# Joint attention of a decoder step: eight identity products on TensorE ahead of each item's scores

## The chip, the cores and the metric

The kernel runs on one core of a Trainium2 chip. Times are microseconds (us) on the device for one execution, start to end. An execution under the profiler is a little longer than the others, so the trace's times are compared with its own total.

## The reference

One layer of a decoder, for a prompt of 1024 tokens and 8 sample tokens. What bears on the change is the dilated window attention: three head groups with (window, dilation) of (128, 1), (512, 4) and (2048, 16), four heads of 64 each, and their outputs combined by their softmax denominators.

```python
def masked_softmax_attend(s, valid, v, spec):
    s = jnp.where(valid, s, -jnp.inf)
    m = jnp.max(s, axis=-1, keepdims=True)
    e = jnp.exp(s - m)
    den = jnp.sum(e, axis=-1, keepdims=True)
    o = jnp.einsum(spec, e / den, v.astype(F32))
    return o, (m + jnp.log(den))[..., 0]
...
def combine_by_denominator(outs, lses):
    w = jax.nn.softmax(jnp.stack(lses), axis=0)
    return jnp.sum(w[..., None] * jnp.stack(outs), axis=0)
```

Ahead of it stands the input projection; behind it the stick-breaking attention, the gates and the output projection, and a mixture of 64 experts.

## The kernel before, in words

The phases run one after another, with all engines together at each border: the projection, `phase_windows` (the one that is changed), `phase_stick`, the gates, the output and routing, the experts. All is float32; large projections split operands into two fp32r parts, `phase_windows` multiplies float32 as it is.

`phase_windows` works on 24 items, one block of 128 queries of one head group each, for its four heads. Items 0 to 7 are of the group with dilation 16, 8 to 11 of the one with dilation 4, first half, 12 to 15 of the dense group, first half; 16 to 19 and 20 to 23 are the second halves. Items 0 to 12 have one block of keys (`nk` = 1, 128 columns), 13 to 23 two (256). Items of the dilated groups read their queries and keys from `turned` with a stride, the dense ones without.

Each engine has a program of its own, a loop over steps `i`, and semaphores order them. In step `i` TensorE writes the scores of item `i+1` (L1190), when DVE has taken those of item `i` out of the single buffer `pS` and masked them; then it transposes the weights of item `i-1` (L1200), when ScalarE has written the exponentials; then it multiplies those of item `i-2` with the values (L1211). In step `i` DVE masks item `i` (L1300), takes its maximum (L1305), which it may write only when the write of item `i-4` to DRAM has landed, since `packed` has four buffers (`PR`); then it negates it, copies the result of item `i-3` into `packed` (L1310), and does scores of the sample tokens in the first 17 steps (L1282, L1285). SyncE issues in step `i` the loads of item `i`'s values, the write of item `i-3`'s `packed` (L1153) and, in odd steps up to 13, four loads for a sample token.

When the last item that covers a tile of 128 tokens is through (item 12 for tile 0, `last_item[0]`), that tile's three parts are loaded (`comb`, L1379, GpSimd), weighed on DVE and ScalarE in step `last_item + 6` (L1361 on), shared out on DVE in step `last_item + 7` (L1352 to L1356), mixed on GpSimd (L1387 to L1394) and transposed on TensorE through `pM` in step `last_item + 9` (`TURN_M`, L1233). GpSimd loads tile t+2's parts after it has mixed tile t.

Of the kernel before, what the change touches and what calls it, by code (L numbers as in the profile page):

```python
# [13 lines left out]
P = 128  # L14
# [35 lines left out]
def rows_of(t):  # L50
    return P if t < NT - 1 else NS
# [19 lines left out]
def build(nc, a, o):  # L71
# [21 lines left out]
    with ExitStack() as ctx:  # L93
        sb = lambda name, shape, dt=F32: ctx.enter_context(nc.sbuf_tensor(name, shape, dt))
        held = []

        def semaphore(name):
            held.append(nc.alloc_semaphore(name=name))
            return held[-1]

        scratch["semaphore"] = semaphore
        ident = sb("ident", [P, P])
        expert_row = sb("expert_row", [1, NBLK + 1], I32)
        slot_info = sb("slot_info", [P, NBLK, 4], I32)
        with ExitStack() as attention:
            turned = attention.enter_context(nc.sbuf_tensor("turned", [P, 20, S], F32))
            phase_project(nc, a, o, scratch, ident, turned)
            branches = ctx.enter_context(ExitStack())
            odT = branches.enter_context(nc.sbuf_tensor("odT", [P, GW // P, T], F32))
            phase_windows(nc, a, o, scratch, ident, turned, odT)  # L110
            oT = branches.enter_context(nc.sbuf_tensor("oT", [P, SBH // 2, T], F32))
            phase_stick(nc, a, o, scratch, ident, turned, oT)

            nc.clear_and_free_semaphores(held)
            nc.all_engine_barrier()
            phase_gate(nc, a, o, scratch, turned, oT, odT)
            branches.close()
            phase_out_route(nc, a, o, scratch, ident, turned, expert_row, slot_info)
        phase_experts(nc, a, o, scratch, ident, expert_row, slot_info)
        phase_finish(nc, a, o, scratch)  # L120
# [869 lines left out]
def phase_windows(nc, a, o, sc, ident, turned, odT):  # L990
# [15 lines left out]
    last_item = [max(i for i, it in enumerate(items) if it["g"] == 0 and it["b"] == t) for t in range(NT - 1)] + [NI]  # L1006
# [8 lines left out]
    ZNEW, ZT, ZE, ZM, EM, SPV, VNEW, PACK, SPV2, PACK2 = 2, 18, 19, 20, 21, 22, 23, 23, 24, 25  # L1015
    WEIGH, MIX, TURN_M = 6, 7, 9
    STEPS = NI + TURN_M + 3

    def tokens(ap, it, first_block, blocks):

        v = ap.rearrange("p (l r) -> p r l", r=STEP[it["g"]])
        return v[:, it["r"], first_block * P:(first_block + blocks) * P]
# [6 lines left out]
    def tile_at(i, step):  # L1029
        return [t for t in range(NT) if last_item[t] + step == i]  # L1030

    with ExitStack() as ctx:
# [37 lines left out]
        pM = ctx.enter_context(nc.psum_tensor("pM_d", [P, 512], F32))  # L1070
# [47 lines left out]
        with nc.Block() as block:  # L1118
# [47 lines left out]
            @block.tensor  # L1166
            def _(pe):
                def sample_values(groups):
                    for g in groups:
                        for h in range(GH):  # L1170
                            for s in range(NS):

                                last = pe.matmul(pX[:NS, (g % 2) * GW + h * HD:(g % 2) * GW + (h + 1) * HD],
                                                 em[:, s, g * GH + h, :], vals[:, s, g, h * HD:(h + 1) * HD],
                                                 start=(s == 0), stop=(s == NS - 1))
                    last.then_inc(spv_done, 1)

                for i in range(-1, STEPS):
                    if i + 1 < NI:

                        it = items[i + 1]
                        g, nk = it["g"], it["nk"]
                        if i >= 0:
                            pe.wait_ge(s_masked, i + 1)
                        for h in range(GH):
                            b = 64 * (h % 2)
                            qt = tokens(turned[b:b + 64, 8 + 2 * g + h // 2, :], it, it["b"], 1)
                            kt = tokens(turned[b:b + 64, 14 + 2 * g + h // 2, :], it, it["b"] - nk + 1, nk)

                            last = pe.matmul(pS[:, h % 2, h // 2, :nk * P], qt, kt, start=True, stop=True)  # L1190
                        last.then_inc(s_ready, 1)
                    j = i - 1
                    if 0 <= j < NI:
                        nk = items[j]["nk"]
                        pe.wait_ge(e_ready, j + 1)
                        if j >= 1:
                            pe.wait_ge(eT_ready, j)
                        for h in range(GH):
                            for k in range(nk):
                                last = pe.transpose(pT[:, (h * nk + k) * P:(h * nk + k + 1) * P], e[:, j % ER, h, k * P:(k + 1) * P], ident[:, :])  # L1200
                        last.then_inc(eT_psum, 1)
                    j = i - 2
                    if 0 <= j < NI:
                        nk = items[j]["nk"]
                        pe.wait_ge(eT_ready, j + 1)
                        pe.wait_ge(v_in[j % 3], v_value[j])
                        if j >= 2:
                            pe.wait_ge(packed_ready, j - 1)
                        for h in range(GH):
                            for k in range(nk):  # L1210
                                last = pe.matmul(pO[:, j % 2, h * HD:(h + 1) * HD], eT[:, j % 2, (h * nk + k) * P:(h * nk + k + 1) * P],  # L1211
                                                 v[:, j % 3, k, h * HD:(h + 1) * HD], start=(k == 0), stop=(k == nk - 1))
                        last.then_inc(pv_done, 1)
                    if i == ZT - 1:
                        pe.wait_ge(z_ready, NU)
                        pe.transpose(pX[:NR, :P], z[:, :], ident[:, :]).then_inc(zt_psum, 1)
                    if i == ZM:
                        pe.wait_ge(se_ready, 1)
                        pe.transpose(pX[:, :NR], zt[:, :P], ident[:NR, :NR]).then_inc(e_psum, 1)
                    if i == SPV:  # L1220
                        pe.wait_ge(em_ready, 1)
                        pe.wait_ge(vals_in, 16 * NU)
                        sample_values((0, 1))
                    if i == SPV2:
                        pe.wait_ge(s_packed_part, 1)
                        sample_values((2,))
                    for t in tile_at(i, TURN_M):
                        m = rows_of(t)
                        pe.wait_ge(mixed_ready, t + 1)
                        if t:  # L1230
                            pe.wait_ge(odT_ready, t)
                        for c in range(2):
                            last = pe.transpose(pM[:, c * P:c * P + m], mixed[:m, t % 2, c * P:(c + 1) * P], ident[:m, :m])  # L1233
                        last.then_inc(mixed_psum, 1)

            @block.scalar
            def _(act):
                for i in range(STEPS):
                    if i < NI:
# [29 lines left out]
            def _(dve):  # L1269
# [17 lines left out]
                dve.wait_ge(consts_in, 32)  # L1287
                for i in range(STEPS):
                    if i < NI:
# [1309 lines left out]
```

## Time and profile before

| | us |
|---|---|
| median of 3 runs | 2373.95 |
| lowest, highest | 2372.28, 2374.68 |
| profiled execution, whole | 2383.18 |
| its span in the trace | 2381.4 |
| `phase_windows`, TensorE's first matmul to the next phase's first | 477.5 to 640.9 |

The span is what the trace covers, 1.8 us less than the whole. The change is in a stage of some 163 us, so it is read by windows and by the engines' timelines there, and not by the page's sums, to which the experts' stage gives most.

### The profile page before, as it was taken

The numbers are of one execution on the slowest core, as the hardware profiler recorded it, in microseconds if no ns is written. First come the engines' busy times: TensorE is split into PE (matmuls) and PEld (weight loads), VectorE is DVE, ScalarE is ACT, GpSimd is POOL, SyncE is SP. The second block draws the span as 40 slices with busy tenths as digits, with TensorE's granted clock in tenths as the row PEclk, the third lists the DMA queues.
The fourth block names the chain that finished last, engine by engine and source line by source line (L and its number), as shares of the span: only waits on it lengthen the run. The fifth ranks groups of instructions, "written<-read, shape, count | busy, mean of one in ns | idle before, by whom it ended". The sixth has DMA issues, their size and how long they took to land. (4 is left out here: it accounts for less than half of the span.)

```text
span 2381.4 us, 38212 instructions
## 1 busy us (share of the span) xinstructions
PE 2162.2 (91%) x13126; PEld 1578.2 (66%) x13126; DVE 1410.3 (59%) x2121; ACT 1037.4 (44%) x1563; POOL 1041.3 (44%) x824
## 2 busy tenths in 40 slices
PE   7999799879499988999899888999999999999994
PEld 6777677667344437888777545677667767767763
DVE  4487678767377753111357526666766766766772
ACT  6221122245266652111234105666666666666662
POOL 2111222122466650011006602677777776777762
PEclk9999899958699999999999898999999999999997
DMA  6577611064345528893352049999999999999995
GB/s 219 177 256 243 223 36 36 30 196 127 133 138 161 165 71 296 274 300 115 109 188 90 20 145 327 323 326 324 323 325 327 322 322 330 320 321 327 324 317 139
DMA packets 180334, 520.57 MB, mean 219 GB/s; under 512 B 22907, under 2 KB 78866, under 8 KB 153790
## 3 DMA queue, kind: packets, MB, share of 16 engines
q1 hardware_dynamic: 133654, 366.37, 44.7%
q0 software_dynamic: 36208, 93.16, 15.5%
q10 hardware_dynamic: 10368, 59.73, 7.5%
q8 instruction: 57, 0.93, 0.2%
q14 instruction: 47, 0.39, 0.1%
HBM read 442.31 MB, written 125.08 MB: 238 GB/s over the span
## 5 line engine op out<-in xcount | busy, mean ns | idle before, releaser
L2465 DVE TENSOR_TENSOR w_gu_lo<-w_e,w_gu_hi 128x2048 fp32r<-128x2048 f32 x132 | 301.9, 2287 | 37.5 <-ACT w_gu_hi L2391 32.7
L2391 ACT ACTIVATE w_gu_hi<-w_e 128x2048 fp32r<-128x2048 f32 x132 | 253.5, 1921 | 43.6 <-DMA w_e<-in_w_e_gate 41.5
L565 PE MATMUL pP<-wring,hT_hi 128*128 128x512 f32 (+2 forms) x576 | 229.4, 398 | 22.7 <-DVE wring L500 13.6
L2327 PE MATMUL pG_e<-w_gu_hi,xT_hi 128*128 128x512 f32 x528 | 232.7, 441 | 1.0 <-issue 1.0
L566 PE MATMUL pP<-wring,hT_hi 128*128 128x512 f32 (+2 forms) x576 | 224.2, 389 | 0.0
L567 PE MATMUL pP<-wring,hT_lo 128*128 128x512 f32 (+2 forms) x576 | 223.5, 388 | 0.0
L2327 PE MATMUL pG_e<-w_gu_hi,xT_lo 128*128 128x512 f32 x528 | 208.8, 396 | 0.0
L2327 PE MATMUL pG_e<-w_gu_lo,xT_hi 128*128 128x512 f32 x528 | 208.2, 394 | 0.0
L2260 POOL DMA_INDIRECT x_scratch<-y_e,target x66 | 107.6, 1630 | 190.4 <-ACT y_tail L2429 190.4
L2246 POOL DMA_INDIRECT rows_tail<-h_scratch,index x66 | 178.2, 2700 | 20.8 <-issue 20.8
L429 ACT ACTIVATE stage<-pP 128x512 f32<-128x512 f32 (+3 forms) x72 | 41.1, 571 | 312.2 <-PE pP L567 303.3
L341 POOL TENSOR_TENSOR wring<-turned,wring 128x512 fp32r<-128x512 f32 (+1 forms) x43 | 71.5, 1697 | 228.6 <-ACT wring L375 228.6
L2473 DVE TENSOR_TENSOR xT_lo<-pX,xT_hi 128x512 fp32r<-128x512 f32 x132 | 90.7, 687 | 115.8 <-ACT xT_hi L2398 115.8
L2428 ACT ACTIVATE y_e<-pY_e,target 128x1024 f32<-128x1024 f32 x66 | 73.7, 1117 | 187.2 <-POOL target L2250 168.3
L2489 DVE TENSOR_TENSOR w_e_lo<-w_e,w_e_hi 128x2048 fp32r<-128x2048 f32 x66 | 150.8, 2285 | 1.4 <-ACT w_e_hi L2405 1.4
L1495 PE MATMUL pG<-hg_hi,wg_hi 128*128 128x344 f32 x384 | 130.2, 339 | 16.3 <-DVE hg_lo L1556 16.3
L1582 POOL TENSOR_TENSOR turned<-halves 128x344 f32<-128x344 f32 x24 | 27.8, 1157 | 261.6 <-DVE halves L1575 261.6
L565 PEld LDWEIGHTS pP<-wring,hT_hi 128*128 128x128 f32 (+1 forms) x576 | 105.8, 184 | 54.4 <-DVE wring L500 14.7
L2317 PE MATMUL pW_e<-w_e,xT_tail 128*32 128x256 f32 x2112 | 129.4, 386 | 0.5 <-DVE xT_tail L2481 0.5
L2242 POOL COPY index<-slot_info 128x2 int32 (+1 forms) x66 | 93.4, 1415 | 80.5 <-POOLq L1738 53.0
L1802 POOL DMA_INDIRECT table_scratch<-token_weight,dest x72 | 76.7, 1065 | 117.9 <-DVE turned L2017 98.1
L2327 PEld LDWEIGHTS pG_e<-w_gu_hi,xT_hi 128*128 128x128 f32 x528 | 99.6, 189 | 40.2 <-issue 28.6
(307 smaller groups left out, 5211.1 us busy)
## 6 DMA issues: line engine op xcount, KB each, us to landing
w_e<-in_w_e_gate SPq DMA_DIRECT2D x66, 1024.0 KB
w_e<-in_w_e_up SPq DMA_DIRECT2D x66, 1024.0 KB
w_e<-in_w_e_down SPq DMA_DIRECT2D x66, 1024.0 KB
turned<-in_cache_sb_kv SPq DMA_DIRECT2D x256, 256.0 KB, 3.1
out<-in_cache_win_kv ACTq DMA_DIRECT2D x8, 4094.0 KB
turned<-in_w_in ACTq DMA_DIRECT2D x56, 256.0 KB, 6.0
turned<-in_w_in SPq DMA_DIRECT2D x16, 512.0 KB, 9.4
out<-in_cache_win_kv ACTq DMA_DIRECT2D x8, 1022.0 KB
```

What stands on the lines that cost most here:

```text
L565: pe.matmul(pP[:m, i % 4, :w], hi, w_hi(u), start=(c == 0), stop=False)
L566: pe.matmul(pP[:m, i % 4, :w], hi, w_lo(u), start=False, stop=False)
L567: last = pe.matmul(pP[:m, i % 4, :w], lo, w_hi(u), start=False, stop=(c == KC - 1))
L1495: pe.matmul(pG[:, i % 2, k, :NC], w_hi[:, r, c, :], hT_hi[:, c, cols], start=(c == 0), stop=False)
L2242: pool.tensor_copy(index[:, r, :], slot_info[:, bass.ds(it * U + j, 1), 0:2]).then_inc(index_ready, 1)
L2246: pool.indirect_dma_start(tail[:, r, :], None, h2_quarters, bass.IndirectOffsetOnAxis(ap=index[:, r, 1:2], axis=0)).then_inc(rows_in[r], 16)
L2260: pool.indirect_dma_start(sc["x2"], bass.IndirectOffsetOnAxis(ap=target[:, r, 0:1], axis=0), y[:, :], None, compute_op=ALU.add).then_inc(y ...
L2317: last = pe.matmul(pW[q * TAIL:(q + 1) * TAIL, :DE], xt[:, r, c, :], w[:, r, k, c * DE:(c + 1) * DE], start=(m == 0), stop=(m == KC // 2 - 1))
L2327: last = pe.matmul(pG[:, :, :], xs[:, r, c, :], ws[:, r, :, c, :], start=(n == 0), stop=(n == 3 * KC - 1))
L2391: act.activation(ghi[:, r, k, :, :].rearrange("p c f -> p (c f)"), w[:, r, k, :], ACT.Copy).then_inc(ghi_ready, 1)
L2465: dve.tensor_tensor(glo[:, r, k, :, :].rearrange("p c f -> p (c f)"), w[:, r, k, :], ghi[:, r, k, :, :].rearrange("p c f -> p (c f)").bitc ...
L2489: dve.tensor_tensor(wlo[:, r, :], w[:, r, 2, :], whi[:, r, :].bitcast(F32), ALU.subtract).then_inc(wlo_ready, 1)
```

## The change

TensorE's program in `phase_windows` gets eight float32 products of the 128 x 128 identity with itself at the head of each step from 0 to 19, written to columns 256 to 383 of `pM`, which nothing reads. They have no semaphore. Step 20 is left out, and the first transpose of a mixed tile, into columns 0 to 255 of `pM`, is in step 21.

```diff
     STEPS = NI + TURN_M + 3
+    FILL, FILLED = 8, last_item[0] + TURN_M - 1
...
                 for i in range(-1, STEPS):
+                    if 0 <= i < FILLED:
+                        for n in range(FILL):
+                            pe.matmul(pM[:, 2 * P:3 * P], ident[:, :], ident[:, :], start=True, stop=True)
                     if i + 1 < NI:
 
                         it = items[i + 1]
```

TensorE's order at the start of the phase, before (pS_d are scores, pT_d transposes, pO_d value products):

```order
L1190 MATMUL pS_d<-turned 128x128 x12
L1200 MATMUL pT_d<-ident,e_win 128x128 x4
L1190 MATMUL pS_d<-turned 128x128 x4
L1200 MATMUL pT_d<-ident,e_win 128x128 x4
L1211 MATMUL pO_d<-v_win,eT 128x64 x4
```

The same place now (lines moved on by one and then by four; L1182 is the identity product):

```order
L1194 MATMUL pS_d<-turned 128x128 x4
L1182 MATMUL pM_d<-ident 128x128 x8
L1194 MATMUL pS_d<-turned 128x128 x4
L1182 MATMUL pM_d<-ident 128x128 x8
L1194 MATMUL pS_d<-turned 128x128 x4
L1204 MATMUL pT_d<-ident,e_win 128x128 x4
L1182 MATMUL pM_d<-ident 128x128 x8
L1194 MATMUL pS_d<-turned 128x128 x4
L1204 MATMUL pT_d<-ident,e_win 128x128 x4
L1215 MATMUL pO_d<-v_win,eT 128x64 x4
L1182 MATMUL pM_d<-ident 128x128 x8
```

Items 0, 1, 2 and 3 had their scores with at most transposes between them; now eight products stand ahead of each but item 0's.

TensorE's order around item 19, before (pX_win<-ident,z_win is a transpose for the sample tokens in step 17):

```order
L1216 MATMUL pX_win<-ident,z_win 96x128
L1190 MATMUL pS_d<-turned 128x256 x4
L1200 MATMUL pT_d<-ident,e_win 128x128 x8
L1211 MATMUL pO_d<-v_win,eT 128x64 x8
L1190 MATMUL pS_d<-turned 128x256 x4
L1200 MATMUL pT_d<-ident,e_win 128x128 x8
```

The same place now:

```order
L1220 MATMUL pX_win<-ident,z_win 96x128
L1182 MATMUL pM_d<-ident 128x128 x8
L1194 MATMUL pS_d<-turned 128x256 x4
L1204 MATMUL pT_d<-ident,e_win 128x128 x8
L1215 MATMUL pO_d<-v_win,eT 128x64 x8
L1182 MATMUL pM_d<-ident 128x128 x8
L1194 MATMUL pS_d<-turned 128x256 x4
```

Between the value products of one step and the scores of the next now stand eight products; the scores' own wait for DVE is behind them.

## Rows read from the trace of the kernel before

**Rows 1.** The page: the span, and the granted clock in 40 slices.
```profile
span 2381.4 us, 38212 instructions
...
PEclk9999899958699999999999898999999999999997
```
**Rows 2.** Busy time by windows: us, PE, PEld, DVE, ACT, POOL, PEclk, DMA share, GB/s.
```profile
478.00:546.00 68.00, 56.33 (x283) 48.72 (x282) 46.87 (x102) 32.86 (x134) 13.27 (x25) 0.50 0.66 199
546.00:576.80 30.80, 28.72 (x205) 23.42 (x203) 22.64 (x52) 19.73 (x61) 8.20 (x13) 1.00 0.43 126
...
896.70:901.00 4.30, 4.28 (x15) 4.28 (x16) 2.73 (x2) 1.31 (x2) 0.00 (x0) 0.50 1.04 409
901.00:906.00 5.00, 5.00 (x34) 5.00 (x33) 0.00 (x0) 0.00 (x0) 0.00 (x0) 1.00 1.03 394
```
**Rows 3.** Timeline of TensorE: start, length, operation, [idle before it and releaser].
```profile
480.85 1.32 PE L1190 MATMUL pS_d<-turned 64*128 64x128 f32 x8 [1.99 <-DVE e_win L1300]
...
491.19 1.33 PE L1190 MATMUL pS_d<-turned 64*128 64x128 f32 x8
492.45 1.11 PE L1200 MATMUL pT_d<-ident,e_win 128*128 128x128 f32 x4
493.36 1.80 PE L1211 MATMUL pO_d<-v_win,eT 128*128 128x64 f32 x8
495.09 1.33 PE L1190 MATMUL pS_d<-turned 64*128 64x128 f32 x8
...
533.33 2.08 PE L1190 MATMUL pS_d<-turned 64*128 64x256 f32 x8 [1.44 <-DVE e_win L1300]
...
547.17 2.19 PE L1190 MATMUL pS_d<-turned 64*128 64x256 f32 x8
...
561.97 2.19 PE L1190 MATMUL pS_d<-turned 64*128 64x256 f32 x8
...
565.02 1.90 PE L1211 MATMUL pO_d<-v_win,eT 128*128 128x64 f32 x16
566.85 1.14 PE L1190 MATMUL pS_d<-turned 64*128 64x256 f32 x8
...
578.71 2.08 PE L1190 MATMUL pS_d<-turned 64*128 64x256 f32 x8 [3.55 <-DVE e_win L1300]
```
**Rows 4.** The waits from 478 to 640: us in total, times, longest.
```profile
DVE packed L1305 <- DMA od_scratch<-packed: 19.5, 8, 5.4
```
**Rows 5.** Timeline of DVE.
```profile
520.71 0.69 DVE L1305 TENSOR_REDUCE packed<-e_win 128x4 f32<-128x512 f32 x1 [2.99 <-DMA od_scratch<-packed]
...
524.92 0.42 DVE L1310 COPY packed<-pO_d 128x256 f32<-128x256 f32 x1
...
529.89 0.69 DVE L1305 TENSOR_REDUCE packed<-e_win 128x4 f32<-128x512 f32 x1 [3.18 <-DMA od_scratch<-packed]
...
564.80 1.22 DVE L1300 TENSOR_TENSOR e_win<-pS_d,band 128x1024 f32<-128x1024 f32 x1
```
**Rows 6.** Timeline of SyncE's DMA queue: start and length of the issue.
```profile
525.37 0.33 SPq L1153 DMA_DIRECT2D od_scratch<-packed  x1
```
**Rows 7.** Timeline of TensorE in two later stages.
```profile
712.20 0.49 PE L985 MATMUL pS<-s_soft,ntri 128*128 128x128 f32 x2
712.52 0.39 PE L986 MATMUL pS<-s_after,nones 128*128 128x128 f32 x2
...
906.31 2.48 PE L1503 MATMUL pG<-oT,turned 128*128 128x344 f32 x8
```
**Rows 8.** Timeline of DVE and GpSimd behind item 19.
```profile
568.52 0.17 DVE L1356 TENSOR_TENSOR wg<-wg,den 128x12 f32<-128x12 f32 x1
...
572.44 0.78 POOL L1379 DMA_DIRECT2D comb<-od_scratch  x1 [0.30 <-POOL mixed L1394]
...
576.49 0.16 DVE L1361 TENSOR_TENSOR top<-comb 128x4 f32<-128x4 f32 x1 [2.63 <-DMA comb<-od_scratch]
```
**Rows 9.** Timeline of TensorE at the start of the next phase.
```profile
640.87 2.93 PE L932 MATMUL pZ<-turned 64*128 64x128 f32 x12 [8.12 <-ACT nones_r L861]
```

## The prediction, made before the changed kernel ran

> **What bounds the kernel now.** The page gives a span of 2381.4 us; TensorE's clock line has its lowest digits, 5 and 6, in the ninth and eleventh of its 40 slices [rows 1]; that is the stage that the change touches, so everything is read from there. The table of windows says more: from 478 to 546 us the granted clock is 0.50 (1.2 GHz) although TensorE is busy 56.3 of 68 us; then 1.00 (2.4 GHz) to 576.8 [rows 2]. So the question is whether TensorE's slow steps set this stage's pace.
>
> Call S(k), T(k), V(k) the scores, the transposes and the value products of item k. TensorE's timeline [rows 3] has S(1) at 480.85, after 1.99 us of idle, so S(0) ended at 478.9; S(13) is at 533.33, S(16) at 547.17, S(19) at 561.97, S(20) at 566.85. From S(1) to S(13) are 12 steps in 52.5 us, 4.37 each. A slow step of one block has S 1.26, T 0.91, V 1.73 from start to start (491.19, 492.45, 493.36, 495.09): 3.9. So TensorE is not quite the pace: the chain of waits has DVE idle for 19.5 us in 8 places before its maximum (L1305), for the write of `packed` to DRAM to land, since only four buffers exist [rows 4].
>
> DVE's timeline shows the loop [rows 5]. The maximum of item 9 starts at 520.71; the copy of item 7's result is at 524.92; the maximum of item 11 starts at 529.89, after 3.18 us of idle. SyncE issues that write at 525.37 [rows 6], and in every second step four loads of sample keys stand ahead of it in the queue. So these two steps cost 4.2 (DVE, from one to the other) + 0.45 (to the issue) + 4.5 (to the landing) = 9.2 us, and none of it is TensorE.
>
> From S(16) on it is different: S(16) to S(19) are three steps in 14.8 us, 4.93 each, and the rows have no idle: S and T 3.05 us (561.97 to 565.02), V 1.83 with the handing over to S(20), at the full clock. Here TensorE sets the pace, or is level with DVE.
>
> **The change part by part.** It removes nothing and moves nothing. It adds 20 x 8 = 160 float32 products of 128 columns, ahead of S(1) to S(20), with no wait of their own; nobody reads what they write. Their costs:
>
> 1. *One product at the full clock.* Each float32 product leaves two records (4 instructions give x8). Eight float32 records of 344 columns at L1503 take 2.48 us, the last with its whole length of some 0.45, so they are 0.29 apart; by columns 128 take 0.108 [rows 7]. The load of 128 columns of weights has to fit beside it: 16 records of V(17), with 64 columns each and thus bound by their loads, take 1.83 us, 0.114 each [rows 3]. So 16 records cost about 1.75 us. The upper bound is the nearest row in shape, L985: 712.20 to 712.52 for two records of 128 columns, 0.160, handing over included; 2.56 us for a step. The lower bound is 0.108, 1.72.
>
> 2. *At the slow clock* V's eight records take 1.73, 0.216 each, so a step's fill is about 3.4 us.
>
> 3. *The clock.* Dense matmuls from 896.7 on are at 0.50 to 901.0 and at 1.00 then [rows 2]: 4.3 us. Here the fill makes TensorE dense from S(0)'s end (478.9) on. I take the clock as high from about 482, and as staying there, since from 546 to 576.8 it stayed high with TensorE busy 28.7 of 30.8 us.
>
> 4. *The first steps.* Fill(0) runs at the slow clock to about 482.1, so S(1) comes 1.2 late; S(2) at 482.1 + 1.25 + 1.75 + 0.1 = 485.2 (1.0 late), S(3) at 488.7 (1.4 late), S(4) at 493.05. V(1), which follows it, ends at 495.6, and item 1's copy, which was at 495.2, is some 0.5 late. That one starts the loop of DVE and DMA: **+0.5 us**.
>
> 5. *S(4) to S(13).* A step on TensorE becomes 1.25 + 0.46 + 0.87 + 1.75 = 4.35 us: T and V halve, S I leave as it is, since its operands are read with a stride (at the full clock the strided S(19), 2.19, is as long as the unstrided S(22) at the slow clock, 2.08, while the unstrided S(20) takes 1.14 [rows 3]). Two steps are 8.7, under the 9.2 of the loop, so they are **hidden**: what hides them is the wait for `packed` to land. What they cost without that cover is 4.35 - 3.9 = 0.45 a step.
>
> 6. *S(13) to S(16)*, 13.84 before. S of items 13 to 15 is not strided: about 1.06 to the next start at the full clock. TensorE's steps become 1.06 + 0.46 + 0.87 + 1.75 + 0.1 = 4.2, 4.2 and, with the eight transposes of item 13, 4.7: 13.1. DVE's are longer, so: **0**.
>
> 7. *S(16) to S(19)*: strided again, and the clock was high before, so nothing is given back. 3.05 + 1.83 + 1.75 = 6.63 for 4.93: three times 1.71 = 5.1. DVE began item 19's mask at 564.80 [rows 5], 0.6 after S(19)'s end (561.97 + 2.19); it now begins right at it: **+4.5**.
>
> 8. *The fill ahead of S(20)* costs 1.75 on TensorE. DVE writes the first tile's shares at 568.52, four steps on item 19's mask; GpSimd mixes, loads tile 2's parts, and DVE waits for them until 576.49 (2.63 idle) [rows 8]. S(20) would end near 575 and DVE's work on item 20 near 579; the shares chain gives 576.49 + 4.5 = 581. Hidden: **0**.
>
> Behind it each tile hangs on the one before (mix, load, weigh, turn), and the next stage starts when the last is done, so the delay is carried to the end. Sum: 0.5 + 4.5 = +5.0 us on the profiled execution's 2383.18 (span 2381.4), so 2388.2 there; on the median of 2373.95, 9 below it, **2379.0**.
>
> A rule that speaks louder against the change: the Trainium skill, page "TensorE: Matmul & The Clock Gate", Part 3, says that a load of weights overlaps matmuls in flight only when their row groups differ. These all use the whole array, so by that rule a record would cost load plus stream, 0.107 + 0.107, and a fill 3.4 us at full clock. The row at L1503 disagrees: 344 columns at 2.4 GHz, streamed twice for float32, are 0.287 of its 0.29 us, which leaves no room for a load.
>
> **The rivals.**
>
> *Dearer fill.* With 0.160 a record, a step of one block is 5.2 us, 10.4 for two, over the loop's 9.2: S(13) comes at about 542 (+8.6), S(16) +10.4, then three steps of 7.45: S(19) +18, and +17 at the end, 2391. With 0.214 (loads not hidden) a step is 6.0: +17, +21.5, and +31 at the end, 2405. It decides from a fill of about 2.0 us on, where two steps pass 9.2. For it: L985's pair. Against: V's and L1503's rows.
>
> *The clock does not rise.* TensorE was busy 83% of the time from 478 to 546 and stayed at 1.2 GHz [rows 2]. Then steps are 7.3 us to S(13) (+32), 8.1 to S(16) (+43), 11 to S(19) (+62): 2436. Against: the fill adds full 128 x 128 matmuls, back to back, as in the stretch before 901 in which the clock rose.
>
> *Not slower.* The delay is given back behind S(19). The place is DVE's wait, from 573.9, for tile 2's parts, 2.63 us: if that landing is set by the DMA queues and not by GpSimd's mix, the chain has 2.6 to give and +5.0 becomes +2.4, 2376.3. It decides when more than 0.3 us is given back. For it: the wait is named as one for a DMA. Against: the load's issue at 572.44 follows GpSimd's mix by 0.3 us [rows 8].
>
> *Faster.* The high clock takes 0.45 from T and 0.86 from V in each of 12 steps, 16 us. It would show if the write landed in under 3.6 us, since then TensorE's 3.9 a step was the pace; but then the fill, 1.75, costs more than the 1.3 that it frees. What stays is a shift of the DMA traffic that shortens the landings: the waits are worth up to 19.5 us, and 5 of them would make 2374 and less.
>
> **How the numbers follow.** I count within 0.2% (4.7 us) as no change: about what this measurement tells. The sum as it stands (+3 to +7): 60%, its middle just on that line, so 32 slower and 28 same. Dearer fill (+7 to +31): 17%, all slower. Clock stays low: 4%, slower. Given back (-4.7 to +3): 12%, same. Faster: 7%. That makes slower 53%, same 40%, faster 7%. The range 2373 to 2391 holds the sum, the case that gives back and the first half of the dearer fill; outside are the unhidden loads, the low clock and the faster case.
>
> **What the profile after would show.** The clock at 1.00 from about 482 us; fill records 0.107 to 0.112 apart; S(13) within 1 us of 533.8; S(16) to S(19) in 20 us and not 14.8; DVE's waits for `packed` about as before; the next stage's first matmul at 645.9 in place of 640.87 [rows 9]. Wrong would be: a clock that falls between fills, S(13) late by 3 or more (then a fill is dearer than the loop hides), or a first matmul of the next stage as early as now (then the tail has slack that I don't see).

## The result and the profile after

The changed kernel takes 2377.76 us (median of 20 runs, 2372.84 to 2384.09) against 2372.76 of before in 20 runs (2367.93 to 2378.27): ratio 1.0022, 95% interval 1.0014 to 1.0030. By the ratio that is 5.2 us slower, 3.3 to 7.1 (the two medians are 5.0 apart); forecast were 5.0. The prediction counted up to 0.2% as no change and gave a slower kernel 53%: the measured 0.22% stands just beyond that line, and its interval lies across it. The changed kernel's one profiled execution has a shorter span than that of before (2376.9 and 2381.4 us), so the page alone would mislead; the stage has to be read.

Below, S(k), T(k) and V(k) are the scores, transposes and value products of item k, as in the prediction, and a fill is the eight products ahead of one item's scores.

The page after, first its span and its clock line (against [rows 1]):

```profile
span 2376.9 us, 38852 instructions
...
PEclk9999899999699998999999898999999999999997
```

The low digits of the ninth and eleventh slices are gone. The windows (us, then PE, PEld, DVE, ACT, POOL, PEclk, DMA share, GB/s) stand against [rows 2]:

```profile
478.00:482.00 4.00, 4.00 (x23) 3.66 (x23) 2.26 (x4) 0.68 (x3) 0.00 (x0) 0.71 0.81 237
482.00:486.00 4.00, 4.00 (x33) 3.64 (x33) 3.83 (x9) 2.30 (x13) 0.00 (x0) 1.00 0.82 247
...
478.00:546.00 68.00, 66.34 (x528) 60.67 (x528) 47.03 (x102) 32.28 (x134) 13.04 (x24) 0.98 0.66 197
546.00:576.00 30.00, 30.00 (x220) 25.23 (x219) 19.65 (x41) 15.30 (x46) 3.65 (x6) 1.00 0.31 95
```

The clock is at 2.4 GHz from about 480 us on, some 4.6 us after the start of S(0), and TensorE is busy 66.3 of 68 us, 10 more than before. DVE's busy time in the window is the same, 47.0 and 46.9: the stage did no more of its work in that time. TensorE's timeline, against [rows 3] (L1182 is the identity product):

```profile
475.65 1.33 PE L1194 MATMUL pS_d<-turned 64*128 64x128 f32 x8 [6.16 <-PEq L273]
476.91 3.67 PE L1182 MATMUL pM_d<-ident 128*128 128x128 f32 x16
480.51 1.32 PE L1194 MATMUL pS_d<-turned 64*128 64x128 f32 x8
...
491.91 1.32 PE L1194 MATMUL pS_d<-turned 64*128 64x128 f32 x8
493.16 0.66 PE L1204 MATMUL pT_d<-ident,e_win 128*128 128x128 f32 x4
493.65 1.00 PE L1215 MATMUL pO_d<-v_win,eT 128*128 128x64 f32 x8
494.49 2.00 PE L1182 MATMUL pM_d<-ident 128*128 128x128 f32 x16
496.43 1.32 PE L1194 MATMUL pS_d<-turned 64*128 64x128 f32 x8
...
533.18 1.14 PE L1194 MATMUL pS_d<-turned 64*128 64x256 f32 x8 [0.87 <-DVE e_win L1304]
...
547.19 2.19 PE L1194 MATMUL pS_d<-turned 64*128 64x256 f32 x8
549.32 1.09 PE L1204 MATMUL pT_d<-ident,e_win 128*128 128x128 f32 x8
550.25 1.90 PE L1215 MATMUL pO_d<-v_win,eT 128*128 128x64 f32 x16
551.98 2.00 PE L1182 MATMUL pM_d<-ident 128*128 128x128 f32 x16
553.91 2.19 PE L1194 MATMUL pS_d<-turned 64*128 64x256 f32 x8
...
567.41 2.19 PE L1194 MATMUL pS_d<-turned 64*128 64x256 f32 x8
...
584.09 1.14 PE L1194 MATMUL pS_d<-turned 64*128 64x256 f32 x8 [2.15 <-DVE e_win L1304]
...
589.80 2.08 PE L1194 MATMUL pS_d<-turned 64*128 64x256 f32 x8 [1.60 <-DVE e_win L1304]
...
647.04 2.94 PE L932 MATMUL pZ<-turned 64*128 64x128 f32 x12 [8.07 <-ACT nones_r L861]
```

Read from start to start. In the first half a step is S 1.25, T 0.49, V 0.84, fill 1.94: 4.52 us with nothing idle in the rows shown; yet S(1) to S(13) is 52.7 us as before, and 0.87 us of idle stands ahead of S(13). From S(16) on, where the scores are read with a stride, a step is 2.13, 0.93, 1.73, 1.93: 6.72 us, where 4.93 stood before, and S(19) comes 91.8 us after S(0) in place of 84.4. The wait for `packed` to land remains, 15.4 us for 19.5 [rows 4]:

```profile
DVE packed L1309 <- DMA od_scratch<-packed: 15.4, 6, 3.4
```

The phase starts 1.9 us earlier in this execution than in that of before, so from here on times are counted from S(0).

### The profile page after: what moved, and what is told of

Its sections match the earlier page's. It is cut to its first block and busy times, and to the rows that moved or that the text cites. A ratio compares the mean times of both kernels' runs of the same rounds, so it can differ in the third digit from the quotient of the medians.

```text
span 2376.9 us, 38852 instructions
## 1 busy us (share of the span) xinstructions
PE 2174.4 (91%) x13446; PEld 1597.5 (67%) x13446; DVE 1408.8 (59%) x2121; ACT 1037.1 (44%) x1563; POOL 1041.9 (44%) x824
## 3 DMA queue, kind: packets, MB, share of 16 engines
q0 software_dynamic: 36208, 93.16, 15.6%
## 5 line engine op out<-in xcount | busy, mean ns | idle before, releaser
L1586 POOL TENSOR_TENSOR turned<-halves 128x344 f32<-128x344 f32 x24 | 27.8, 1159 | 264.0 <-DVE halves L1579 264.0
L565 PEld LDWEIGHTS pP<-wring,hT_hi 128*128 128x128 f32 (+1 forms) x576 | 106.0, 184 | 52.5 <-DVE wring L500 12.1
L2246 POOL COPY index<-slot_info 128x2 int32 (+1 forms) x66 | 93.4, 1415 | 79.6 <-POOLq L1742 52.2
L2409 ACT ACTIVATE w_e_hi<-w_e 128x2048 fp32r<-128x2048 f32 x66 | 125.3, 1899 | 0.0
```

What stands on the lines that cost most here:

```text
L565: pe.matmul(pP[:m, i % 4, :w], hi, w_hi(u), start=(c == 0), stop=False)
L2246: pool.tensor_copy(index[:, r, :], slot_info[:, bass.ds(it * U + j, 1), 0:2]).then_inc(index_ready, 1)
```

## The experiments

Twelve runs followed on three chips, four at a time; three of them (e5, e9, e10) repeat the kernel before or the changed one for one more profile. The phase and its marks come from TensorE's timeline of each: the starts of S(13), S(16), S(19) and of the next phase's first matmul (L932), less the start of S(0). "Time" is the change of the whole kernel against before on the same chip: the ratio less one, and the ends of its 95% interval, by the median of before there (2372.8 us for the change itself; 2373.0 for e1 to e4, 2381.6 for e6 to e8, 2384.6 for e11 and e12).

| kernel | S(13) | S(16) | S(19) | phase | time, us |
|---|---|---|---|---|---|
| before | 55.8 | 69.6 | 84.4 | 163.3 | |
| e5, before again | 59.0 | 72.5 | 88.1 | 167.3 | |
| e9, before, third | 58.3 | 71.4 | 87.5 | 169.0 | |
| after | 57.5 | 71.5 | 91.8 | 171.4 | +5.2 (3.3 to 7.1) |
| e10, after again | 58.1 | 72.1 | 92.4 | 172.0 | |
| e1, products in steps 0 to 15 | 59.1 | 72.8 | 87.5 | 168.8 | +1.7 (-1.9 to 5.2) |
| e2, products in steps 16 to 19 | 57.5 | 70.1 | 91.8 | 170.0 | +4.0 (0.7 to 7.4) |
| e3, six buffers | 48.9 | 62.7 | 77.5 | 159.3 | -11.9 (-15.9 to -8.1) |
| e4, six buffers and the change | 56.2 | 69.6 | 89.8 | 168.0 | +3.6 (0.9 to 6.4) |
| e6, four products a step | 55.4 | 69.3 | 86.9 | 167.3 | -1.2 (-4.3 to 1.7) |
| e7, transposes as fill | 58.0 | 72.0 | 92.0 | 170.6 | +4.0 (1.4 to 6.7) |
| e8, six buffers, products in steps 0, 1 | 49.9 | 61.5 | 76.2 | 154.7 | -11.7 (-15.5 to -7.9) |
| e11, six buffers, four products to S(13) | 46.3 | 57.7 | 73.9 | 152.2 | -13.8 (-18.1 to -9.5) |
| e12, six buffers, two products to S(13) | 46.9 | 57.5 | 73.8 | 151.4 | -12.4 (-16.9 to -7.6) |

**One part of the change alone: e1 and e2.** The condition on the step is all that differs.

```diff
-                    if 0 <= i < FILLED:
+                    if 0 <= i < 16:
```

> Identity products in steps 0 to 15 only, none ahead of S(17) to S(20). Measure: the phase, from its first scores to the next phase's first matmul (163.3 us before, 171.4 with the change). Theory A (the cost is exposed where TensorE sets the pace, three strided steps from S(16), and a little at the start; the loop of DVE and the landing of packed hides the rest): S(16) 1.9 late as with the change, S(16) to S(19) back at 14.8 us, phase 165.2, time +2 us on before. Rival B (each of the 20 fills costs its share wherever it stands): phase 163.3 + 16/20 of 8.1 = 169.8, time +6.5.

S(16) to S(19) took 14.75 us, as the theory has it, for 20.2 with the change. The phase is 168.8 and not 165.2, but that of before is as long in its other two profiles (167.3, 169.0). The time is +1.7, with an interval that holds zero and the change's own +5.2 too, so that the time alone doesn't show what is saved. Rival B's +6.5 lies outside the interval, but it was worked out from the 8.1 us between two single profiles; with the measured 5.2 us it wants +4.2, and the time doesn't exclude that. What speaks against it are the marks: without a fill in them, S(16) to S(19) are back at their 14.8 us.

```diff
-                    if 0 <= i < FILLED:
+                    if 16 <= i < FILLED:
```

> Identity products in steps 16 to 19 only (ahead of S(17) to S(20)). Theory A: the clock rises as before the change, about 68 us into the phase; S(16) to S(19) takes 20.2 us for 14.8, phase 163.3 + 6.2 = 169.5, time +6 us. Rival B: 4/20 of 8.1, phase 164.9, +1.6.

These four of the twenty fills cost most of what all do: the phase is 170.0, 3.5 above the mean of before (166.5, below) where the change is 5.2 above it, and the time +4.0 (expected +6). In time rival B isn't excluded, neither with its +1.6 nor with 4/20 of 5.2, +1.0. The marks again place the cost: S(16) to S(19) took 21.7 us for 14.8 to 16.1 before, since three fills stand there and the clock fell for the first of the steps. TensorE's timeline of e2:

```profile
546.45 2.19 PE L1194 MATMUL pS_d<-turned 64*128 64x256 f32 x8 [0.70 <-DVE e_win L1304]
548.57 1.97 PE L1204 MATMUL pT_d<-ident,e_win 128*128 128x128 f32 x8
550.33 2.52 PE L1215 MATMUL pO_d<-v_win,eT 128*128 128x64 f32 x16
552.69 2.00 PE L1182 MATMUL pM_d<-ident 128*128 128x128 f32 x16
```

The transposes take 1.76 to the next start and not 0.93: the slow clock, with 0.70 us of idle ahead. That is one thing that the fill gives back in the changed kernel: in the six profiles with fills up to S(16) (after, e1, e4, e6, e7, e10) the granted clock is 1.00 from S(16) to S(19), while it falls there in five of the eight others (e2, e5, e9, e11, e12). So before takes 15.6 us (e5) and 16.1 us (e9) for these three steps, and 14.8 in the first profile.

**The loop's buffers: e3 and e4.** On the kernel before and on the changed one:

```diff
-    PR = 4
+    PR = 6
```

> The kernel before with six buffers of packed in place of four, no identity products. Theory A (the wait for packed to land paces S(1) to S(13)): DVE's waits for it, 19.5 us, go to under 3, and TensorE at the slow clock takes over with 3.9 us a step: S(1) to S(13) 47 to 49 us for 52.5, phase about 159, time -4 us. Rival C (the landing is only put down as the releaser; another wait, the loads of values or sample keys, takes its place): S(1) to S(13) stays at 52 us and the phase at 163.

> The changed kernel with six buffers of packed. Theory A: the cover of the fill is gone, TensorE's 4.52 us a step sets S(1) to S(13): 54 us, no faster than with four buffers (52.7), phase 171 to 172, so that the fill costs 12 us against the same kernel without it (e3) where it cost 8 with four buffers. Rival C: all as with the change, and e3 as before: 8 us between them.

TensorE's timeline of e3 (six buffers alone) and then of e4:

```profile
499.58 1.33 PE L1190 MATMUL pS_d<-turned 64*128 64x128 f32 x8
500.84 1.12 PE L1200 MATMUL pT_d<-ident,e_win 128*128 128x128 f32 x4
501.75 1.81 PE L1211 MATMUL pO_d<-v_win,eT 128*128 128x64 f32 x8
503.48 1.31 PE L1190 MATMUL pS_d<-turned 64*128 64x128 f32 x8
```

```profile
502.16 1.32 PE L1194 MATMUL pS_d<-turned 64*128 64x128 f32 x8
503.42 0.66 PE L1204 MATMUL pT_d<-ident,e_win 128*128 128x128 f32 x4
503.91 1.00 PE L1215 MATMUL pO_d<-v_win,eT 128*128 128x64 f32 x8
504.75 2.00 PE L1182 MATMUL pM_d<-ident 128*128 128x128 f32 x16
506.68 1.32 PE L1194 MATMUL pS_d<-turned 64*128 64x128 f32 x8
```

In e3 a step is 3.90 us (S 1.26, T 0.91, V 1.73 at the slow clock), with no idle; S(1) to S(13) is 45.3 us and DVE's wait for `packed` is no longer among its waits. Rival C is out: that wait did set the pace. S(1) to S(13) is even below the 47 to 49 us expected, and the time is -11.9 us where -4 was expected. In e4 the same steps are 4.52, and S(1) to S(13) is 51.4 us, 6.1 more than in e3, where with four buffers the change adds nothing (52.7 and 53.2 with it; 52.5, 55.3 and 54.6 without). With four buffers the change has little cover left: S(4) to S(10) is 27.1 and 27.4 us in its two profiles and 27.1 in e4, which is TensorE's own pace, and six buffers take only 1.3 to 1.8 us off its S(1) to S(13). The expected 54 was 2.6 too much: it counted twelve full steps, and the first two and the last are shorter. With the cover gone the change costs 168.0 - 159.3 = 8.7 us of phase, expected were 12, and 15 us of time (+3.6 against -11.9). e3's gain in time, 8 to 16 us, is more than its phase shows against the mean of before (166.5 - 159.3 = 7.2): the rest was not traced.

**Chance or kernel: e5, e9, e10.**

> The kernel before once more, for one more profile of it. In the profiled execution of before the stage of the output projection and the routing took 257 us, in the five others seen so far 246 to 248, while its phase of windows is 163.3. Theory: that is chance of one execution, and not of the kernel before: here the phase is 163 to 164 again and that stage 246 to 249. Rival: the changed kernels shorten that stage by their earlier work, and it is 257 again.

The stage of the output projection and the routing (L1821 to the experts' first matmul) took 257 us again, so "chance of one execution" was wrong; but the rival is wrong too: versions with products or six buffers took 254 to 257 on this chip and the third, and 246 to 248 in the first profile of the change and in e1 to e4. It goes with the chip, as far as the record names one, which is why spans from different chips can't be set against each other here. The record names no chip for the first profile of before; its 257 us in this stage speak for another one than that of e1 to e4. The profiler by itself adds little: the changed kernel's profiled execution, 2378.69 us, lies among its twenty, so the 9 us of before's profile over its median are rather another chip's than the profiler's; that is argued and not shown. No profile of before comes with the chip of e1 to e4 on record, and their phases are set against before across chips. And the phase was 4 us longer than in the first profile, which led to the next pair.

> The kernel before, a third profile, on the same chip as the next. Its phase was 163.3 and 167.3 us in the two profiles so far, S(13) at 55.8 and 59.0. Theory H (the landings of packed vary from execution to execution, so the loop's pace does): phase again between 163 and 168.

> The changed kernel, a second profile. Theory H with A: S(1) to S(13) 52 to 55 us, S(16) to S(19) 20.2 again, S(20) to the end of the phase 71 to 73, phase 170 to 175, and 5 to 6 above the mean of the three profiles of before. Rival: S(16) to S(19) also varies, by over 1 us.

The phase of before is 163.3, 167.3 and 169.0, mean 166.5 (the third a little beyond the range expected), that of the change 171.4 and 172.0, mean 171.7: 5.1 more, close to the measured 5.2. S(13) of before varies by 3.2 us with the landings; S(16) to S(19) of the change is 20.2 both times.

**Half the fill: e6.**

```diff
-    FILL, FILLED = 8, last_item[0] + TURN_M - 1
+    FILL, FILLED = 4, last_item[0] + TURN_M - 1
```

> The change with four products ahead of each item in place of eight. Theory A (a fill costs what it takes on TensorE where TensorE sets the pace): S(16) to S(19) 14.8 + 3 x 0.95 = 17.6 us, with eight 20.2; the clock still rises early; S(13) about 57; phase about 167, time +3 us. Rival: the fill's cost is a handing over between operations and not its length, so that four cost nearly what eight do: S(16) to S(19) 19 or more.

TensorE's timeline of e6:

```profile
489.57 1.11 PE L1182 MATMUL pM_d<-ident 128*128 128x128 f32 x8
490.61 1.32 PE L1194 MATMUL pS_d<-turned 64*128 64x128 f32 x8
```

Four products cost 1.04 us from start to start, eight 1.94: 0.225 each and 0.14 once, for handing over to the scores. S(16) to S(19) took 17.5 (expected 17.6). In time it can't be told from before: -1.2 us (-4.3 to 1.7), and the +3 expected is outside the interval. S(13) came at 55.4, not about 57, early enough to make up for most of what S(16) to S(19) cost. The clock rose early but was low for some 7 us twice, from about 512 and 532 us, each time after a wait with TensorE idle.

**What lifts the clock: e7.** Sixteen transposes of the identity, which have one record each, in place of eight products with two.

```diff
-                            pe.matmul(pM[:, 2 * P:3 * P], ident[:, :], ident[:, :], start=True, stop=True)
+                            pe.transpose(pM[:, 2 * P:3 * P], ident[:, :], ident[:, :])
```

> The change with 16 transposes of the identity in place of the eight products: also 16 records on TensorE, of 0.11 us each at the full clock and 0.22 at the slow one. Theory D (the clock answers to how busy TensorE is, whatever it runs): clock high from about 5 us on, all as with the change, phase 170 to 172. Rival E (transposes do not lift the clock; the Trainium skill, page TensorE: Matmul & The Clock Gate, Part 4, says that transposes don't count as busy in the same way; whether they do here, no run has shown): clock at 0.50 to S(13) and beyond, 7.3 us a step, S(13) at 90 or more, phase over 220.

The windows of e7:

```profile
480.00:546.00 66.00, 62.30 (x513) 55.90 (x513) 44.18 (x98) 31.72 (x128) 13.03 (x24) 1.00 0.64 191
```

The clock is high as with products, from some 4 us after S(0), and the phase is 170.6. Rival E falls. Theory D is right that transposes do as well as products, but how busy TensorE is doesn't decide by itself: in e8, below, it is busy without a pause at 0.50. The Trainium skill, page "TensorE: Matmul & The Clock Gate", Part 4, says that transposes don't bring the full clock; this trace disagrees, with transposes that alternate with scores and value products. A stretch of transposes alone was not tried.

**Getting more from a clock that is up: e8, e11, e12.** All with six buffers; e8 keeps the products of steps 0 and 1 only, e11 four and e12 two products in steps 0 to 12 (`if 0 <= i < 2:`, and `if 0 <= i < 13:` with `FILL` 4 and 2).

> Six buffers of packed, and identity products ahead of S(1) and S(2) only. Theory F (once high, the clock holds through steps in which TensorE is busy some 75% of the time): TensorE's step is 2.6 us, DVE's 3.0 to 3.3 sets the pace, S(1) to S(13) about 40 us (six buffers without products 45.3), S(20) at 76 to 78 (82.4), phase 153 to 155, time -18 us on before if the rest follows as with six buffers. Rival G (the clock falls back within a few steps without products): S(1) to S(13) 44 to 45 us and the phase 160, as with six buffers alone.

Windows of e8:

```profile
476.00:485.00 9.00, 8.04 (x52) 7.07 (x53) 7.46 (x14) 3.78 (x17) 0.00 (x0) 0.88 0.69 220
485.00:525.00 40.00, 40.00 (x208) 36.05 (x205) 31.39 (x74) 23.34 (x95) 13.04 (x24) 0.50 0.80 237
```

The clock rose with the two fills and fell when they ended; then TensorE was busy for 40 of 40 us at 1.2 GHz: rival G, as far as the steps go (44.9 us for S(1) to S(13)). The clock rose before S(14) with no product ahead of it, and the phase came to 154.7, as theory F had it, for another reason; the time is -11.7 us and not -18.

> Six buffers of packed and four products ahead of S(1) to S(13) only. Theory I (without waits for packed the four products hold the clock, and a step costs TensorE 3.63 us where it cost 3.9 at the slow clock): S(1) to S(13) 43 us (six buffers alone 45.3), S(16) to S(19) 14.8, phase 157, time -14 us on before. Rival G (the clock falls back in between): S(1) to S(13) 48 or more, phase 162, no faster than before less 6.

> Six buffers of packed and two products ahead of S(1) to S(13). Theory I: if the clock holds, TensorE's step is 3.2 us and DVE's about the same, S(1) to S(13) 39 to 41, phase 153 to 155, time -18 us on before. Rival G: the clock is low for most of S(3) to S(13), a step 3.9 + 0.9 = 4.8 us, S(1) to S(13) 55, phase 168, and the time that of before or more.

Windows of e11, in the same stretch:

```profile
485.00:525.00 40.00, 39.10 (x309) 34.85 (x309) 33.36 (x76) 24.24 (x99) 13.04 (x24) 1.00 0.80 249
```

TensorE is no busier than in e8, and the clock is high throughout. S(1) to S(13) is 42.4 us (43 expected), in e12 43.6 (39 to 41 expected; by the windows the clock was low for the first 8 us and for 7 later). In both S(16) to S(19) took 16.2 us and not 14.8, as the clock fell for the first of these steps. The phases are 152.2 (157 expected) and 151.4 (153 to 155 expected). In time both are faster than before, -13.8 and -12.4 us, but their intervals and e3's and e8's lie over each other: that the products add something to the six buffers is seen in the phase (159.3 in e3, on another chip), not shown in the time. The lowest ratio here is e11's, 0.9942 (0.9924 to 0.9960).

## Why the prediction was right

- *Cost of a fill.* 1.72 to 2.56 us were the bounds, 1.75 the choice; measured 1.80 and 0.14 of handing over (e6). (The value products from which the choice was read, behind S(19), are item 16's and not item 17's; the number stands.) The upper bound, L985's pair, had just that handing over in it. Loads are hidden behind the stream: the rival of 0.214 a record is out, 0.112 was seen.
- *Clock.* High from 480, which is 4.6 us after S(0), as taken (482, with S(0) at 477.5), and in both profiles of the change never low until after S(22). The rival "does not rise" is out. Eight products a step don't always keep it: in e1 it was low for some 3 us from 516, after 1.1 us of idle between 512 and 514.
- *First steps.* S(1) was 1.3 us late against the mean of before (1.2 forecast) and S(4) 2.4 (1.9 forecast). Of that, 0.1 is left at S(13) (means 57.8 and 57.7): the 0.5 of the sum can't be told from the spread of before, 3.2 us.
- *S(4) to S(13) hidden.* Right, and shown by e3 and e4: with the wait taken away the same fills cost 6.1 us. A step was 4.52 for 4.35; two are 9.04, just under the loop's 9.2, so the cover was thinner than the sum had it: 0.16 us and not 0.5. From S(4) to S(10) TensorE itself set the pace of the changed kernel: 27.1 and 27.4 us, where before took 27.8 to 28.4.
- *S(13) to S(16).* +0.6 (13.5 mean before, 14.05 after) for a forecast of 0. TensorE's three steps are 4.3, 4.9 and 4.8, not below DVE's.
- *S(16) to S(19).* The main term, 5.1: measured 20.2 less 15.5, the mean of three profiles, is 4.7 (the sum counted 4.5 of the 5.1, the rest as DVE's slack); the marks of e1 and e2 place it there. Each step was 6.74 for 6.63, but before isn't always 14.8, as its clock falls at times.
- *Fill ahead of S(20) hidden, delay carried to the end.* S(19) to the next phase is 79.6 in both profiles after and 78.9, 79.2 and 81.5 before: nothing was added, and the rival "not slower" got at most 0.3 us back on the mean. What varies there is the clock at S(22) and S(23). Where both take 2 us and more (e1, e3, e9), S(19) to the end is 81.3 to 81.8; with one or neither of them slow, in the other eleven profiles, 77.7 to 80.4. That is read off the profiles and not tried by itself.

The sum of these on the means, 0.1 + 0.6 + 4.7 - 0.3 = 5.1, is close to the measured 5.2. That the number came out so close is partly luck: single profiles of before differ by up to 5.7 us in this phase, and the forecast took one of them, the shortest. Its marks show it. The next stage's first matmul was to come 168.4 us after S(0) (645.9 less 477.5) and came at 171.4 and 172.0; S(13) was to come at 56.3, within 1 us, and came at 57.5 and 58.1. The differences, which make the forecast of the time, fit better than the marks, and the terms that missed (0.1 for 0.5, 0.6 for 0, 4.7 for 4.5, -0.3 for 0) cancel.

## What to carry to other kernels

Filler on TensorE lifts the clock cheaply where TensorE waits, but a faster clock is only worth what TensorE's steps are worth there: here another loop, four buffers and a DMA landing, set the pace, and the clock's gain had nowhere to go. Look for that loop first: six buffers gave 12 us, filler on four buffers cost 5. Filler belongs only in steps where its length fits into a wait, and should end where TensorE sets the pace and the kernel's own work has the clock up: from S(16) to S(19) the fills here were mostly paid for (4.7 of the 5.8 us of three). That ending it there gains time is seen in the marks (e1) and not shown in the time of the whole.

## What the runs showed of the hardware

- TensorE busy for 40 of 40 us at the slow clock (e8), and for 39.1 of 40 at the full one with four identity products a step (e11): a row of busy time doesn't tell which clock was granted.
- Transposes among the other work raised and held the clock as products did (e7: 1.00 from 480 to 546 us).
- Scores whose operands are read with a stride gain nothing from the full clock: for 128 columns 1.26 us to the next start in before at the slow level and 1.25 after at the full one, while the length of unstrided ones of 256 columns goes from 2.08 to 1.14. A stride of 4 is no better than one of 8 (the steps of the two dilated groups in `turned`): items 8 to 11 take 1.30 to 1.31 us at either level, while unstrided item 12 takes 1.23 and 0.72.
- A stage that no version changes, the output projection and the routing, took 246 to 248 us on one chip (e1 to e4) and 254 to 257 on two others (e5 to e12); the kernel before took 2373.0, 2381.6 and 2384.6 us on the three.
